# Gate placement: left one-hots made in fp32 on DVE, right rows shared between ACT and GpSimd

## What is computed

```
s = einsum('nhpc,hpkc->nhpk', q, keys)            # scores against 2 x 128 half keys per head
sv, si = top_k(s, 16)                             # best 16 of each half
cv, ci = top_k(sv[0][:, None] + sv[1][None, :], 16)
expert = i1 * 128 + i2                            # i1, i2: the two half keys of each choice
gate = softmax(cv)
out = sum over heads and choices: gate * gelu(u[expert] . h) * v[expert]
```

## Time and profile before

| | us |
|---|---|
| median of 3 runs | 3403.36 |
| lowest, highest | 3396.24, 3411.25 |
| profiled execution | 3394.97 |
| its span | 3393.4 |
| placing of gates, within the span | 696.4 to 1108 |
| expert stage, within the span | 1153 to 3393 |

### The profile page before, as it was taken

How to read it: one execution, slowest core, us unless ns; L and a number is a source line. 1 busy time by engine, 2 the same in 40 slices (tenths; PEclk the granted TensorE clock), 3 DMA queues, 4 the chain that set the end, 5 groups by cost and what they waited for, 6 DMA issues and landing times.

```text
span 3393.4 us, 43989 instructions
## 1 busy us (share of the span) xinstructions
PE 3066.7 (90%) x16658; PEld 2343.7 (69%) x16658; DVE 2404.3 (71%) x4977; ACT 933.2 (28%) x1271; POOL 1502.4 (44%) x1188
## 2 busy tenths in 40 slices
PE   8899969877888399999999999999999999889985
PEld 1466644455555389987888878888788888677784
DVE  1232324988888888887778777777777777777786
ACT  0111101278888222221222122222122222111121
POOL 0010010055555244455665556655556565655542
PEclk9899989999999699999999999999999999999997
DMA  9611141012223478889999999999999999898872
GB/s 356 203 63 62 56 154 51 13 56 106 106 106 149 181 263 283 288 279 342 351 380 341 368 326 366 366 353 358 354 348 360 364 364 339 326 334 303 319 271 111
DMA packets 305917, 858.68 MB, mean 253 GB/s; under 512 B 25377, under 2 KB 108833, under 8 KB 303985
## 3 DMA queue, kind: packets, MB, share of 16 engines
q0 software_dynamic: 151344, 551.09, 44.3%
q1 hardware_dynamic: 154333, 305.79, 25.4%
q10 hardware_dynamic: 108, 0.22, 0.0%
HBM read 793.86 MB, written 63.15 MB: 253 GB/s over the span
## 4 chain that ended last, share of the span: by engine, by line
PE 48%; DMA 6%; DVE 6%; POOL 3%; issue 2%; ACT 1%; POOLq 0%; DVEq 0%; SPq 0%
PE y_ps L1856 22%; PE a_ps L1837 18%; PE picked_ps L1874 5%; DMA shared<-in_peer_u,ids 3%; PE uT_ps L1824 3%; DMA shared<-in_peer_v,ids 3%; POOL quad L1468 2%; POOL shared L1457 2%; DVE shared L1653 1%; DVE shared L1670 1%; DVE uT_lo L1611 1%; DVE shared L1640 1%; DVE v_lo L1631 0%; DVE m_lo L1626 0%; ACT uT_hi L1538 0%
## 5 line engine op out<-in xcount | busy, mean ns | idle before, releaser
L1457 POOL DMA_INDIRECT shared<-in_peer_u,ids x512 | 623.4, 1218 | 628.0 <-DVE acts L1653 528.9
L1653 DVE CUSTOM_DVE_ANT_0 shared<-shared 128x1024 f32<-128x1024 f32 x512 | 618.0, 1221 | 161.9 <-DMA shared<-in_peer_u,ids 161.5
L1837 PE MATMUL a_ps<-h_hi,uT_lo 128*128 128x320 f32 x2048 | 644.0, 314 | 1.7 <-DVE h_lo L1771 1.7
L1837 PE MATMUL a_ps<-h_lo,uT_hi 128*128 128x320 f32 x2048 | 633.9, 310 | 0.0
L1837 PE MATMUL a_ps<-h_hi,uT_hi 128*128 128x320 f32 x2048 | 633.7, 309 | 0.0
L1856 PE MATMUL y_ps<-v_hi,m_lo 128*128 128x512 f32 x1280 | 520.0, 406 | 88.1 <-DVE m_lo L1626 54.0
L1640 DVE TENSOR_TENSOR shared<-shared,y_ps 128x512 f32<-128x512 f32 x640 | 428.3, 683 | 156.3 <-PE y_ps L1856 155.5
L1856 PE MATMUL y_ps<-v_lo,m_hi 128*128 128x512 f32 x1280 | 511.3, 399 | 0.0
L1856 PE MATMUL y_ps<-v_hi,m_hi 128*128 128x512 f32 x1280 | 508.5, 397 | 0.0
L1468 POOL DMA_INDIRECT quad<-in_peer_v,idsT x384 | 425.7, 1109 | 117.1 <-issue 117.1
L1837 PEld LDWEIGHTS a_ps<-h_hi,uT_lo 128*128 128x128 f32 x2048 | 386.4, 189 | 7.4 <-issue 2.1
(11 more groups left out here) (180 smaller groups left out, 4103.7 us busy)
## 6 DMA issues: line engine op xcount, KB each, us to landing
shared<-in_peer_u SPq DMA_DIRECT2D x128, 512.0 KB, 7.5
v_all<-in_peer_v SPq DMA_DIRECT2D x128, 512.0 KB, 7.6
gate_blocks<-dense SPq DMA_DIRECT2D x10, 4096.0 KB, 12.5
gates<-gate_blocks SPq DMA_DIRECT2D x64, 640.0 KB, 22.3
w_ada<-in_w_ada SPq DMA_DIRECT2D x12, 2048.0 KB, 11.0
x_in<-in_x_prompt SPq DMA_DIRECT2D x16, 512.0 KB, 4.5
shared<-in_peer_u,ids POOLq DMA_INDIRECT x512, 8.4
shared<-in_w_in SPq DMA_DIRECT2D x8, 768.0 KB, 12.6
```

The lines of the kernel that those rows point to most:

```text
L1457: pool.indirect_dma_start(out=rows[n % 4], out_offset=None, in_=u_table if n < DOTS else v_table, in_offset=bass.IndirectOffsetOnAxis(ap=i ...
L1653: nc.vector.tensor_tensor_reduce(out=rows[n % 4], in0=rows[n % 4], in1=token_row, scale=1.0, scalar=0.0, op0=ALU.mult, op1=ALU.add, accum_ ...
L1837: last = nc.tensor.matmul(a_ps[n][:, 0:GROUP], lhs[s][:, k, :], rhs[:, k, tok], start=k == 0 and m == 0, stop=k == KD - 1 and m == 2)
```

## The change

Three pieces of work change hands:

- `left` is no longer made by ACT out of a bf16 `left_hot`. DVE compares in fp32 (`leftT` with a new ramp `iota_left`) and writes `left` in its final order. `left_hot` is gone.
- `right` is no longer made by Pool alone. ACT makes the rows of tokens 0 to 5 of a batch, one instruction for each token, 128 elements, with the gate of that token as the instruction's per-partition scale. Pool makes tokens 6 and 7 in one instruction of 256 elements.
- The semaphores follow: `right` counts twice a batch (after ACT's fourth and sixth row), `right_rest` counts Pool, PE's first half waits for `left` and the first four rows only. DVE's `left` waits with `wait_for_placed`, and `right_hot` waits for ACT's and Pool's rows of batch b-2. `take_slots` has three copies instead of two.

In ACT's queue a placing period begins before and after as follows. `q`, `qT` are the query copies of the next tile, `gateT`, `keyT`, `leftT` and `rightT` the tile's own gates and keys.

The diff, with `BY_ACT = 6`; where a wait on `slotsT` counted two a tile it now counts three:

```diff
         total = sbuf(nc, mem, "total", [P, HEADS])
         slots = sbuf(nc, mem, "slots", [P, 3, HEADS, TOPK])
-        keyT = sbuf(nc, mem, "keyT", [P, 2, P], BF16)
+        leftT = sbuf(nc, mem, "leftT", [P, P])
+        rightT = sbuf(nc, mem, "rightT", [P, P], BF16)
         gateT = sbuf(nc, mem, "gateT", [P, P])
-        left_hot = [sbuf(nc, mem, f"left_hot{s}", [P, NKEYS, BATCH], BF16) for s in range(2)]
         left = [sbuf(nc, mem, f"left{s}", [P, BATCH, NKEYS]) for s in range(2)]
         right_hot = [sbuf(nc, mem, f"right_hot{s}", [P, NKEYS, BATCH], BF16) for s in range(2)]
...
         row_loaded = [S.u0, S.u1, S.u2, S.u3, S.u4, S.u5, S.u6, S.u7]
         BATCHES = P // BATCH
+        BY_ACT = 6
         key4 = best_key[:, :, :].rearrange("p (h s) k -> p h s k", s=2)
         block = mem.enter_context(nc.Block())
...
             pool.iota(iota_rank[:, :, :], pattern=[[1, TOPK], [0, TOPK]], base=0, channel_multiplier=0,
                       allow_small_or_imprecise_dtypes=True).then_inc(S.iota, 1)
+            pool.iota(iota_left[:, :], pattern=[[1, NKEYS]], base=0, channel_multiplier=0,
+                      allow_small_or_imprecise_dtypes=True).then_inc(S.iota, 1)
             pool.iota(iota_keys[:, :, :], pattern=[[1, NKEYS], [0, BATCH]], base=0, channel_multiplier=0,
                       allow_small_or_imprecise_dtypes=True).then_inc(S.iota, 1)
...
 
                 d = t - FIRST_DENSE
-                pool.wait_ge(S.slotsT, t * 2 + 2)
+                pool.wait_ge(S.slotsT, t * 3 + 3)
                 for b in range(BATCHES):
                     wait_for_placed(pool, d, b)
                     pool.wait_ge(S.right_hot, d * BATCHES + b + 1)
                     nc.gpsimd.tensor_tensor(
-                        right[b % 2][:, :, :], right_hot[b % 2][:, :, :].rearrange("p i t -> p t i"),
-                        gateT[:, b * BATCH:(b + 1) * BATCH].rearrange("p (t o) -> p t o", o=1)
-                        .to_broadcast([P, BATCH, NKEYS]), ALU.mult).then_inc(S.right, 1)
+                        right[b % 2][:, BY_ACT:, :], right_hot[b % 2][:, :, BY_ACT:].rearrange("p i t -> p t i"),
+                        gateT[:, b * BATCH + BY_ACT:(b + 1) * BATCH].rearrange("p (t o) -> p t o", o=1)
+                        .to_broadcast([P, BATCH - BY_ACT, NKEYS]), ALU.mult).then_inc(S.right_rest, 1)
 
             def period(choose, done, prepare):
...
             def take_slots(t):
                 act.wait_ge(S.slotsT_ps, t + 1)
-                nc.scalar.activation(keyT[:, :, :], x_ps[:, 0:2, :], ACT.Copy).then_inc(S.slotsT, 1)
+                nc.scalar.activation(leftT[:, :], x_ps[:, 0, :], ACT.Copy).then_inc(S.slotsT, 1)
+                nc.scalar.activation(rightT[:, :], x_ps[:, 1, :], ACT.Copy).then_inc(S.slotsT, 1)
                 nc.scalar.activation(gateT[:, :], x_ps[:, 2, :], ACT.Copy).then_inc(S.slotsT, 1)
 
...
 
                 act.wait_ge(S.slotsT_ps, t + 1)
+                act.sem_inc(S.slotsT, 1)
                 if ORDER[t] < MIXED:
                     nc.scalar.activation(idsT[:, ORDER[t], :], x_ps[:, 0, :], ACT.Copy).then_inc(S.slotsT, 1)
...
                     nc.scalar.activation(gatesT[:, ORDER[t], :], slots[:, 2, :, :].rearrange("p h k -> p (h k)"), ACT.Copy)\
                         .then_inc(S.slotsT, 1)
+
+            def right_rows(d, b):
+
+                act.wait_ge(S.right_hot, d * BATCHES + b + 1)
+                wait_for_placed(act, d, b)
+                for n in range(BY_ACT):
+                    last = nc.scalar.activation(right[b % 2][:, n, :], right_hot[b % 2][:, :, n], ACT.Copy,
+                                                scale=gateT[:, b * BATCH + n:b * BATCH + n + 1])
+                    if n in (3, BY_ACT - 1):
+                        last.then_inc(S.right, 1)
 
             def widen_keys(t, s):
...
                                      key4[:, :, s, :].rearrange("p h (a o) -> p h a o", o=1)
                                      .to_broadcast([P, HEADS, TOPK, TOPK]), ACT.Copy).then_inc(S.key_wide, 1)
-
-            def left_rows(d, b):
-
-                act.wait_ge(S.left_hot, d * BATCHES + b + 1)
-                wait_for_placed(act, d, b)
-                nc.scalar.activation(left[b % 2][:, :, :], left_hot[b % 2][:, :, :].rearrange("p i t -> p t i"),
-                                     ACT.Copy).then_inc(S.left, 1)
 
             def take_gates(d, b):
...
                 for b in range(BATCHES):
                     if placed is not None:
-                        left_rows(placed - FIRST_DENSE, b)
+                        right_rows(placed - FIRST_DENSE, b)
                         if b:
                             take_gates(placed - FIRST_DENSE, b - 1)
...
             def hot_rows(d, b):
 
-                keys_iota = iota_keys[:, :, :]
-
-                def key(n):
-                    return keyT[:, n, b * BATCH:(b + 1) * BATCH].rearrange("p (o t) -> p o t", o=1)\
-                        .to_broadcast([P, NKEYS, BATCH])
-                wait(dve, S.right, d * BATCHES + max(b - 1, 0))
-                nc.vector.tensor_tensor(right_hot[b % 2][:, :, :], key(1), keys_iota, ALU.is_equal)\
-                    .then_inc(S.right_hot, 1)
-                wait(dve, S.left, d * BATCHES + max(b - 1, 0))
-                nc.vector.tensor_tensor(left_hot[b % 2][:, :, :], key(0), keys_iota, ALU.is_equal)\
-                    .then_inc(S.left_hot, 1)
+                tokens = slice(b * BATCH, (b + 1) * BATCH)
+                wait(dve, S.right, (d * BATCHES + max(b - 1, 0)) * 2)
+                wait(dve, S.right_rest, d * BATCHES + max(b - 1, 0))
+                nc.vector.tensor_tensor(
+                    right_hot[b % 2][:, :, :],
+                    rightT[:, tokens].rearrange("p (o t) -> p o t", o=1).to_broadcast([P, NKEYS, BATCH]),
+                    iota_keys[:, :, :], ALU.is_equal).then_inc(S.right_hot, 1)
+                wait_for_placed(dve, d, b)
+                nc.vector.tensor_tensor(
+                    left[b % 2][:, :, :],
+                    leftT[:, tokens].rearrange("p (t o) -> p t o", o=1).to_broadcast([P, BATCH, NKEYS]),
+                    iota_left[:, :].rearrange("p (o i) -> p o i", o=1).to_broadcast([P, BATCH, NKEYS]),
+                    ALU.is_equal).then_inc(S.left, 1)
 
             def period(choose, done, prepare):
...
                 n = d * BATCHES + b
                 pe.wait_ge(S.left, n + 1)
-                pe.wait_ge(S.right, n + 1)
                 for g in range(2):
-
+                    pe.wait_ge(S.right, n * 2 + g + 1)
+                    if g:
+                        pe.wait_ge(S.right_rest, n + 1)
                     pe.wait_ge(S.placed, n * 2 + g + 1)
                     for j in range(4):
```

More of the change, by code:

```diff
@@ L703, in routing @@
     S = sems(nc, "route", "passed consts wq experts_in iota h2 keys_ps keysT q_ps q qT_ps qT scores "
-                               "scores_used shifted exp gate_ready keyed slotsT_ps slotsT left_hot left "
-                               "right_hot right place_ps placed out0 out1 best_key key_wide first_keyed dve expert picked row_in used "
+                               "scores_used shifted exp gate_ready keyed slotsT_ps slotsT left "
+                               "right_hot right right_rest place_ps placed out0 out1 best_key key_wide first_keyed dve expert picked row_in used "
                                "u0 u1 u2 u3 u4 u5 u6 u7")
@@ L743, in routing @@
         iota_keys = sbuf(nc, mem, "iota_keys", [P, NKEYS, BATCH], BF16)
+        iota_left = sbuf(nc, mem, "iota_left", [P, NKEYS])
         s_ps = psum(nc, mem, "s_ps", [P, HP, NKEYS])
@@ L958, in _ @@
             PER_TILE = 139
-            dve.wait_ge(S.iota, 2)
+            dve.wait_ge(S.iota, 3)
             dve.wait_ge(S.keysT, 1)
@@ L1124, in rows @@
                     if b == 0 and done is not None:
-                        dve.wait_ge(S.slotsT, done * 2 + 2)
+                        dve.wait_ge(S.slotsT, done * 3 + 3)
                     if placed is not None:
@@ L1212, in period @@
                     if done is not None:
-                        pe.wait_ge(S.slotsT, done * 2 + 2)
+                        pe.wait_ge(S.slotsT, done * 3 + 3)
                     turn(prepare, 0)
```

## The result

The changed kernel took 3442.26 us (median; 3439.12 to 3447.02), the kernel before 3399.8 us beside it: ratio 1.0121, 95% interval 1.0106 to 1.0136. It is slower by 1.2%; 3446 was forecast. The profiled execution has a span of 3437.5 us.

The account below looks back on a forecast made before the run. ACT's unbroken batches were taken to bound the placing stage; 0.65 us more a batch gave about 43 us over five tiles, other parts 0, so 3403.4 + 43 = 3446 us; likeliest range 3430 to 3460, 8 in 10 3390 to 3460.

Parts of the forecast that it names:

- ACT bounds the stage: Placing stage: ACT, never idle from a tile's third batch to its second `key_wide`, sets the time; both loops run through its batches.
- Six copies, taken at 2.61 us: ACT, each batch: high end, no overlap between copies, 435 ns each; 0.65 us more than the `left` pass of 1.96 us.
- the low end of the bound: ACT's copies overlapping, with the strided read: 0.34 us each, six 2.07 us, 0.11 more than `left`.
- The strided read: ACT reading every eighth bf16 element: 1.81 ns an element plus 0.11 us fixed time, against 0.83 ns for a plain read.
- Rival B: ACT's short copies escape the strided cost, with no operand cost; ACT gets cheaper and the kernel faster, 3369 us; chance 0.12.
- The sum, 43 us: Loss over five tiles: 2 x 8.9 us in the first loop plus 3 x 8.7 in the second, less the last pass.
- DVE's parts at nothing: DVE: fp32 `left` 0.55 us longer, 8.8 us a tile, stretching of 13.7 us a tile gone; both off the chain, 0.
- DVE's floor: DVE's own least time for a tile: 59.3 us, with 3 us for collisions with Pool, against 66.2 us now.
- DVE's new wait at nothing: DVE's `left` waiting for PE's placing of batch b-2: selection pieces may take 5.8 us, the longest is 4.2; cost 0.
- Pool at nothing: Pool keeping two of eight rows: its instruction falls from 2.7 us to 0.6 to 1.2, with slack before and after; 0.
- the wrong loop: First loop: first `right_hot`, ACT's batches, second `key_wide`, DVE's tail, next tile's `right_hot`; 8.9 us a tile, counted for two tiles.
- the second loop: ACT's first group follows PE's product, made after PE's last placement, which waited for `dense`; 8.7 us a tile, three tiles.

Follow-up runs that it names:

- 6: Kernel before, with ACT making `left` in eight copies of 128 elements instead of one pass of 1024, no scale operand: 3448.21 us, ratio 1.0124.
- 1: Changed kernel with ACT's six copies a batch made without the gate as scale operand: 3399.26 us, ratio 0.9991.
- 3: Changed kernel with ACT making four of eight `right` rows and Pool four: 3391.04 us, ratio 0.9956.
- 4: Changed kernel with ACT making all eight `right` rows and Pool none: 3497.36 us, ratio 1.0274.
- 10: Changed kernel with ACT making five `right` rows and Pool three: 3405.93 us, ratio 1.0013.
- 5: Changed kernel with ACT making no `right` rows and Pool all eight, DVE still making `left` in fp32: 3442.5 us, ratio 1.0112.
- run 2: Changed kernel with ACT making its six rows in one strided pass of 768 elements without the gate: 3377.68 us, ratio 0.9924.
- 7: Changed kernel with three buffers of `left`, so DVE's `left` waits for PE's placing of batch b-3 instead of b-2: 3439.73 us, ratio 1.0104.
- run 8: Changed kernel with the gate multiplied into `left` by eight DVE tensor_scalars, `right` copied ungated, ACT's six rows in one pass: 3418.99 us, ratio 1.0048.

## Why the prediction was right

- **ACT bounds the stage.** Shown from both sides: its batch made longer with nothing else changed gave the loss (6), its batch restored with everything else changed took the loss away (1), and the time follows the number of its rows down to five, and half as steeply to four (3, 4, 10). It is not the only bound near: with no rows on ACT at all DVE and Pool together take as long (5).
- **Six copies, taken at 2.61 us, measured 2.48.** The direction and nearly all of the size were right, the reason for the size was not. I took the high end on the ground that nothing overlaps. Plain short copies do overlap: 0.32 us apart for 0.46 us of duration, which is the low end of the bound (0.34). The gate operand lengthens each by 0.09 us on top. The Trainium skill, "ScalarE: Activation LUTs", section "What ACT_TABLE_LOAD costs", gives about 93 ns for each pointer operand and about 93 ns of overlap between neighbours. Run 1 agrees on the operand; the overlap, mean duration less step, is more: 0.53 - 0.41 = 0.12 us with the operand, 0.46 - 0.32 = 0.14 without. The estimate that the prediction made beside that page, 0.42 us a copy and 2.51 for six, was nearer than the term that it took (the sum with 2.51 is 36.6 us, though, not below 36, and six copies at the low end are 2.05 us, not 2.07).
- **The strided read** at 1.81 ns an element held: 0.11 + 768 x 1.81 ns gave 1.50 us, and the pass of run 2 moves the next start by 1.50; for 128 elements it gave 0.34 and run 1 has 0.32. Rival B rested on the opposite.
- **The sum, 43 us, measured 38.2** between the two marks. The term that was mis-sized is the copies: 0.65 us a batch more than `left` was taken, 2.48 - 1.96 = 0.52 measured. That makes 13 x 0.52 + 0.5 = 7.3 and 14 x 0.52 - 0.4 = 6.9 us a tile; five of them, less the last pass, are 35. Seen were 6.7, 10.0, 7.4 and 7.1. The 10.0 is a tile that the prediction counted in the wrong loop, as is shown below. The difference of the medians, 42.5 us, is nearer to the forecast than the stage is; part of that is luck, since the median of the kernel before was 3399.8 beside this kernel and 3402 to 3405 beside the experiments.
- **DVE's parts at nothing.** `left` at 1223 ns (1.23 taken) and the end of the stretching were both hidden, as forecast. That collisions would move on to the selection's own operations (956 ns for L1053, 413 before) I had allowed for with 3 us in DVE's floor; it cost nothing here and decided run 5. The waits for `key_wide` stayed at 2.1 us; I had expected them to grow, but DVE's slack went into the new wait: with it loosened they grew to 4.7 us (7).
- **DVE's new wait at nothing.** 84.3 us of waiting appeared, and run 7 shows them free.
- **Pool at nothing.** Its instruction, taken at 0.6 to 1.2 us, measured 1.76 behind DVE's `left`; DVE's `right_hot` waited for it 0.7 us in all.

The tile in the wrong loop is the second. ACT's third group there, before and after:

```profile
790.60 2.09 ACT L908 ACTIVATE left<-left_hot 128x1024 f32<-128x1024 bf16 x1 [0.36 <-DVE left_hot L1116]
```

```profile
798.06 0.60 ACT L879 ACTIVATE qT<-x_ps 128x512 f32<-128x512 f32 x1 [0.78 <-PE x_ps L1182]
798.55 2.60 ACT L904 ACTIVATE right<-right_hot,gateT 128x128 f32<-128x128 bf16 x6
```

The tile's first comparison stood at 779.59 and now at 783.58. Before, ACT's first group began 3.7 us after it and the third, held by DVE, 11.0 us; now the first begins 6.8 us after it, behind PE's product, and the third 15.0 us. So the second tile has gone over to the second loop, which costs some 3 us beyond its copies.

## What to carry to other kernels

Before work is taken off an engine because it looks stretched or busy, find the engine whose work has no gaps between the points where the others wait for it; here the stretching of DVE by Pool was 61 us of busy time, of which 9 us of the kernel's came back when it was taken away. Splitting one pass on that engine into several pays the fixed start each time, and a per-partition operand pays again; count both from the distance of starts, not from durations. When a share of work is moved between engines, run the split as a series: the best one lies where two engines wait for each other a little.

## What had not been expected of the hardware

- A DVE tensor_scalar of 128 fp32 elements with two per-partition operands moved the next start by 0.30 us (run 8); one of 128 uint32 elements with an immediate, `digits`, by 0.14.
- In the middle of the tiles the granted TensorE clock was 0.92 to 0.94 where it had been 0.97 to 1.00, with the same products: PE waited longer between them (103.6 us ahead of the placing products, 86.2 before). Some of its time was thus spent at the lower level, 1.2 GHz, and not at 2.4; since PE did not end last, none of the loss is put down to it.
